# The next sample's 32 compression phases dealt out between the units of a sample's attention

## The reference, cut to what matters

```python
kc = compress_blocks(full_cmp[:, :, 0], cmp_pe[0], cmp_w1[0], cmp_b1[0], cmp_w2[0])
vc = compress_blocks(full_cmp[:, :, 1], cmp_pe[1], cmp_w1[1], cmp_b1[1], cmp_w2[1])
...
p_cmp = masked_softmax(s_c, dist_c >= 0)
o_cmp = jnp.einsum('bghtn,bngd->btghd', p_cmp.astype(vc.dtype), vc)
...
imp = selection_importance(jnp.sum(p_cmp, axis=2), nsb)
...
_, idx = lax.top_k(score, n_sel)
...
o = (gates[:, :, 0, :, :, None] * o_cmp + gates[:, :, 1, :, :, None] * o_slc + gates[:, :, 2, :, :, None] * o_win)
```

## Time and profile before

| | us |
|---|---|
| device time, median of three runs (lowest to highest) | 3484.95 (3482.47 to 3486.91) |
| the profiled execution's own time | 3489.78 |
| its span | 3488.0 |
| TensorE busy | 3230.7 (93%) |
| VectorE busy | 1371.0 (39%) |
| ScalarE busy | 989.5 (28%) |
| GpSimd busy | 922.9 (26%) |
| moved by DMA | 329.68 MB |

### The profile page before, as it was taken

The page is one execution under the profiler, slowest core; times in us unless marked ns, Lnnn a source line. Parts: engine busy times, 40 slices in busy tenths (PEclk is TensorE's granted clock), DMA queues, the critical chain, the costliest instruction groups (busy, mean ns, idle before and its releaser), DMA issues.

```text
span 3488.0 us, 58282 instructions
## 1 busy us (share of the span) xinstructions
PE 3230.7 (93%) x23752; PEld 2946.3 (84%) x23752; DVE 1371.0 (39%) x2939; ACT 989.5 (28%) x1634; POOL 922.9 (26%) x403
## 2 busy tenths in 40 slices
PE   7999998899999999999989999888888887899997
PEld 6999967699998999989987667776677775799997
DVE  3111324411124221241036657766667664411124
ACT  2111210221113211122124444444444443311222
POOL 2333320233334333344220001111111110233332
PEclk9999999999998999989957999899899989899998
DMA  6232221222322223232430004454444544222321
GB/s 140 70 95 73 80 68 52 66 76 70 97 66 76 81 70 97 58 84 70 130 111 1 1 1 152 164 194 160 172 147 156 193 171 120 73 77 80 91 62 35
DMA packets 365938, 329.68 MB, mean 95 GB/s; under 512 B 60469, under 2 KB 345397, under 8 KB 347920
## 3 DMA queue, kind: packets, MB, share of 16 engines
q1 hardware_dynamic: 322264, 180.59, 18.7%
q0 software_dynamic: 21216, 139.89, 11.3%
q10 hardware_dynamic: 22240, 6.17, 0.9%
HBM read 320.39 MB, written 14.58 MB: 96 GB/s over the span
## 4 chain that ended last, share of the span: by engine, by line
PE 79%; issue 8%; DVE 7%; ACT 2%; POOL 1%; DMA 1%; DVEq 0%; POOLq 0%; ACTq 0%
PE psum L1590 51%; PE psum L1854 4%; PE psum L1856 3%; PE psum L1855 3%; PE psum L1910 3%; PE psum L1821 3%; PE psum L2026 2%; PE psum L1943 2%; PE psum L1921 2%; DVE x_lo L1130 1%; PE psum L1874 1%; POOL w_sp L616 1%; PE psum L1584 1%; ACT w_room L913 1%; DMA ring<-in_cache_l_cmp_kv,idxc 1%
## 5 line engine op out<-in xcount | busy, mean ns | idle before, releaser
L1590 PE MATMUL psum<-x_hi,w_sp 128*128 128x288 f32 x5888 | 1042.5, 299 | 38.4 <-DVE x_lo L1130 24.3
L616 POOL TENSOR_TENSOR w_sp<-ring,w_sp 128x2048 fp32r<-128x2048 f32 (+2 forms) x162 | 680.3, 4199 | 1298.9 <-ACT w_sp L759 1298.9
L1590 PEld LDWEIGHTS psum<-x_hi,w_sp 128*128 128x128 f32 x5888 | 880.9, 191 | 43.0 <-issue 23.7
L1590 PE MATMUL psum<-x_lo,w_sp 128*128 128x288 f32 x2944 | 637.5, 299 | 0.0
L1590 PE MATMUL psum<-h_hi,w_sp 128*128 128x288 f32 (+1 forms) x2816 | 502.0, 298 | 0.0
L1590 PEld LDWEIGHTS psum<-x_lo,w_sp 128*128 128x128 f32 x2944 | 481.7, 191 | 0.0
L1590 PEld LDWEIGHTS psum<-h_hi,w_sp 128*128 128x128 f32 (+1 forms) x2816 | 416.5, 188 | 10.5 <-issue 10.1
L1106 DVE TENSOR_TENSOR h_hi<-act_tmp,psum 128x576 f32 (+1 forms) x88 | 66.4, 754 | 861.3 <-ACT act_tmp L798 861.3
L759 ACT ACTIVATE w_sp<-ring 128x2048 fp32r<-128x2048 f32 (+1 forms) x162 | 275.6, 1701 | 445.3 <-PE psum L1590 406.7
L1854 PE MATMUL psum<-ch_hi,w_hi 128*128 128x256 f32 (+1 forms) x1056 | 316.3, 300 | 38.3 <-DVE ch_lo L1263 38.1
L1855 PE MATMUL psum<-ch_lo,w_hi 128*128 128x256 f32 (+1 forms) x1056 | 313.2, 297 | 0.0
(11 more groups left out here) (271 smaller groups left out, 3931.2 us busy)
## 6 DMA issues: line engine op xcount, KB each, us to landing
ring<-in_w_ffn_in SPq DMA_DIRECT2D x168, 512.0 KB
ring<-in_w_ffn_out SPq DMA_DIRECT2D x32, 640.0 KB
ring<-in_w_ffn_out SPq DMA_DIRECT2D x32, 384.0 KB
ring<-in_w_ffn_out SPq DMA_DIRECT2D x32, 320.0 KB
ring<-in_cache_l_win_kv SPq DMA_DIRECT2D x8, 1024.0 KB, 5.5
out<-in_cache_l_win_kv SPq DMA_DIRECT2D x1, 8064.0 KB
ring<-in_w_in_even SPq DMA_DIRECT2D x6, 1024.0 KB
ring<-in_w_in_odd SPq DMA_DIRECT2D x6, 1024.0 KB
```

The lines of the kernel that those rows point to most:

```text
L616: pool.tensor_tensor(w_sp[:, u % 2, 1, 0:w], ring[:, slot, 0:w], w_sp[:, u % 2, 0, 0:w].bitcast(F32), ALU.subtract).then_inc(lo_ready, 1)
L1590: last = pe.matmul(out[:, c], lhsT, rhs[:, c * TH:(c + 1) * TH], start=start, stop=stop)
```

## The change

The work of each sample stays, and its place in the queues moves. While a sample's attention runs, the 32 phases of the *next* sample run between its steps: `PRO = 5` phases at the boundary between two samples, and `PER` phases in the 12 units. The loop now covers six samples, from attention to boundary; the seventh turn and the last attention are written out. The merge of a sample lies in the boundary after it.

```diff
-NSLOT = 6
+NKEY = 3
...
+        PRO = 5
+        PER = [3, 3, 3] + [2] * 9
```

TensorE's new order (`scores` one unit ahead of the output in place of two):

```diff
+            def boundary(b, o, first=False, more=True):
+                keys(b, o, WINC)
+                if more:
+                    phase(b, o + 1, 0)
+                    phase(b, o + 1, 1)
+                pe.wait_ge(q_set, b * 4 + (o * 4 + 4))
+                scores(b, o, 0)
+                if more:
+                    phase(b, o + 1, 2)
+                second_layer(b, o)
+                if more:
+                    phase(b, o + 1, 3)
+                transposes(b, o, 0)
+                if more:
+                    phase(b, o + 1, 4)
+                if not first:
+                    output_transpose(b, o - 1)
...
+            def attend(b, o, more=True):
+                at = PRO
                 for a in range(SU):
+                    if a + 1 < SU:
+                        scores(b, o, a + 1)
+                    for n in range(PER[a]):
+                        if more:
+                            phase(b, o + 1, at)
+                        at += 1
+                        if n == 0:
+                            output(b, o, a)
+                            if a + 2 in CHUNK:
+                                keys(b, o, a + 2)
+                        if n == 1 and a + 1 < SU:
+                            transposes(b, o, a + 1)
```

Beside phase i of the next sample, `along` on ScalarE makes the high part of phase i + 3, and `along` on VectorE turns the chunk of phase i + 3 and makes the low part of phase i + 2. ScalarE copies both halves of the keys (`k_round`, semaphore `k_act`) into one buffer in place of two. Gelu runs twice per sample, on 4 x 255 columns, at the boundary; ScalarE's order there:

```diff
+            def boundary(b, o, first=False, more=True):
+                first_half_of(b, o, 7)
+                k_round(b, o, WINC)
+                gelu_of(b, o, 0)
+                if more:
+                    along(b, o + 1, 0)
+                gelu_of(b, o, 1)
+                if more:
+                    along(b, o + 1, 1)
+                if not first:
+                    weights(b, o - 1)
+                exp_unit(b, o, 0)
```

```diff
+            for s in range(DB):
+                key_load(s, 3)
+                if s + 1 < DB:
+                    chunk_loads(s + 1, 2)
+                    chunk_loads(s + 1, 3)
+                for c in range(4, 8):
+                    key_load(s, c)
+                if s + 2 < DB:
+                    chunk_loads(s + 2, 0)
+                key_load(s, 8)
+                if s + 1 < DB:
+                    key_load(s + 1, 1)
+                    key_load(s + 1, 2)
+                if s + 2 < DB:
+                    chunk_loads(s + 2, 1)
```

More of the change, by code:

```diff
@@ L705, in _ @@
             pool.wait_ge(idx_ready, 5)
[L707 to L739, removed]
+            def gather(dst, rows, at, full):
+                pool.indirect_dma_start(out=dst, out_offset=None, in_=rows,
+                                        in_offset=bass.IndirectOffsetOnAxis(ap=at, axis=0)).then_inc(full, 16)
@@ new lines, in _ @@
+            pool.wait_ge(hb_ready, 1)
+            pool.wait_ge(w1_high, 2)
+            pool.wait_ge(w1_low[0], 1)
+            pool.wait_ge(w1_low[1], 1)
+            chunk_loads(0, 0)
+            pool.wait_ge(blk_done, blk_pos["odd"] + 11)
+            chunk_loads(0, 1)
+            for c in range(2):
+                pool.wait_ge(kv_out[c], 6 * 16)
+            key_load(0, 1)
+            pool.wait_ge(t_ready, R0)
+            key_load(0, 2)
+            chunk_loads(0, 2)
+            chunk_loads(0, 3)
@@ L1040, in _ @@
+            for i in range(3):
+                high_chunk(0, 0, i)
+            for i in range(XS):
+                along(0, 0, i)
+            boundary(0, 0, first=True)
+            with act.Fori(0, DB - 2) as b:
+                attend(b, 0)
+                boundary(b, 1)
+            attend(DB - 2, 0, following=False)
+            boundary(DB - 2, 1, more=False)
+            attend(DB - 2, 1, more=False)
+            weights(DB - 1, 0)
             norm(4, after=3)
@@ L1556, in _ @@
+            for i in range(3):
+                turn(0, 0, i)
+            for i in range(2):
+                low(0, 0, i)
+            for i in range(XS):
+                along(0, 0, i)
+            boundary(0, 0, first=True)
+            with dve.Fori(0, DB - 2) as b:
                 step.off = b * STEPS
                 n_before = step.n
-                attend(b, False)
-                compress(b, 1)
-                first_keys(b, 1)
+                attend(b, 0)
+                boundary(b, 1)
@@ L2085, in _ @@
-            compress(0, 0)
-            with pe.Fori(0, DB - 1) as b:
-                attend(b)
-                compress(b, 1)
-            attend(DB - 1)
-            output_transpose(DB - 1)
+                    each, n = key_count(c)
+                    pe.wait_ge(key_full[c % NKEY], b * each + (o * each + n))
+                if a == 4:
+                    pe.wait_ge(imp_done, b + (o + 1))
+                pe.wait_ge(k_act, b * SR + (o * SR + 2 * c))
+                for gp in range(2):
+                    for p in range(4):
+                        last = pe.transpose(bank(gp)[:, p * P:(p + 1) * P],
+                                            key_slots[c % NKEY][:, p * ROW + gp * P:p * ROW + (gp + 1) * P], ident)
+                    last.then_inc(t_ready, 1)
@@ new lines, in scores @@
+            def scores(b, o, a):
+                pe.wait_ge(soft, b * SU + (o * SU + NU + a - 1))
+                for gp in range(2):
+                    if a == CMPU:
+                        w, rhs = NB, kc[:, gp, :]
+                        pe.wait_ge(cv_sb, b * 2 + (o * 2 + 3))
+                    elif a in CHUNK:
+                        w, rhs = 512, kTc[:, gp, :]
+                        pe.wait_ge(k_act, b * SR + (o * SR + 2 * CHUNK[a] + gp + 1))
+                    else:
+                        w, rhs = DT, kT[:, 0 if a == SLCN else 1, gp, bass.ds(b * DT + (TP + o * DT), DT)]
+                    if a in (WINN, SLCN):
+                        last = pe.matmul(bank(4 + a % 2)[:, 0:w], qb[:, gp, :], rhs, start=gp == 0, stop=gp == 1)
+                    else:
+                        rows = slice(gp * 64, (gp + 1) * 64)
+                        last = pe.matmul(bank(4 + a % 2)[rows, 0:w], qb[:, gp, rows], rhs, start=True, stop=True)
+                last.then_inc(sc_ready, 1)
@@ new lines, in parts, with transposes @@
+            def parts(a):
+                if a == CMPU:
+                    return [(P, 0, P), (NB - P, P, NB - P)]
+                if a in CHUNK:
+                    return [(P, p * P, P) for p in range(4)]
+                return [(DT, 0, DT)]
+            def transposes(b, o, a):
+                n = o * SU + NU + a
+                if a == CMPU:
+                    pe.wait_ge(p_norm, b + (o + 1))
+                else:
+                    pe.wait_ge(p_ready, b * SU + (n + 1))
+                pe.wait_ge(pt_sb, b * SU + n)
+                for j, (m, c0, w) in enumerate(parts(a)):
+                    last = pe.transpose(bank(6)[0:m, j * P:(j + 1) * P], sp3[:, a % 3, c0:c0 + w], ident)
+                last.then_inc(ptp_ready, 1)
@@ L2092, in _ @@
+            pe.wait_ge(soft, NU)
+            for i in range(XS):
+                phase(0, 0, i)
+            boundary(0, 0, first=True)
+            with pe.Fori(0, DB - 2) as b:
+                attend(b, 0)
+                boundary(b, 1)
+            attend(DB - 2, 0)
+            boundary(DB - 2, 1, more=False)
+            attend(DB - 2, 1, more=False)
+            output_transpose(DB - 1, 0)
             pe.wait_ge(ot_done, DB + 1)
```

587 lines of the change are left out of this document (282 added, 305 removed).

## The result

The changed kernel takes 3404.43 us (median of four runs, 3400.93 to 3409.14), the kernel before 3483.78 us beside it: a ratio of 0.977, 95% interval 0.9755 to 0.9789. The forecast was 3403 us. The profiled execution took 3409.1 us, its span 3407.3, TensorE's mean clock 0.946.

The account below looks back on a forecast made before the run. The sample loop, 862.3 us, was taken to lose 25 us of each 107.6 us period to waiting or half clock. Periods of 96 us bring it to 780 us, 82 less, so 3403 us; 8-in-10 range 3345 to 3460 us.

Parts of the forecast that it names:

- The stage: Sample loop, 862.3 to 780 us: first compression 51.1, first turn 87, five of 96, seventh 92, last attention 70.
- rival 4: Phases among attention work: no overlap, TensorE waits for phases as for units; 107 us a period, 3485 us; chance 0.04.
- Units 5 to 11 are TensorE's: Later attention units: TensorE sets the time, 6.1 us per full unit, 39 us in all.
- The boundary and units 0 to 4 are VectorE's, 53 us: Start of a period: VectorE's 41 us of work plus four added waits make 53 us; TensorE has some 45.
- The wait for the weights: Boundary: VectorE waits 4.6 us for ScalarE's merge weights, an 8.6 us chain less 4 us of VectorE work.
- rival 2: Boundary chain longer, with Gelu at 2.0 us and hops of 0.4: 103 us a period, 3456 us; chance 0.20.
- The jump: Loop's jump back to its start: 3.6 us each, placed on VectorE's chain at the boundary.
- rival 1: Whole period: TensorE becomes the bound if weights come early and hops overlap; 88 us a period, 3343 us; chance 0.17.
- Three key slots just fit; piece 8 is 2 us late: Key gathers: landing 6.1 us at the median fits a 6.1 us unit; piece 8, behind two chunk gathers, some 2 us late.
- Rival 3: Pieces 4 to 8: late key slots decide, slower; at an 11 us landing time 884 us of stage, 3507 us; chance 0.09.
- The rule that spoke against it: Key gathers beside VectorE's phases: VectorE's two-port mode locks out GpSimd's descriptor writing; rows show 0.2 us at the median.
- The last attention: Final sample, no phases to hide behind: pieces 4 to 8 take 5.2 us each; 70 us, where 57.8 was.

Follow-up runs that it names:

- the weights' runs: Changed kernel with ScalarE making the merge's weights ahead of Gelu: 3367.88 us (0.9671 of the kernel before); with TensorE's loop also written out: 3358.87 us (0.9649).
- e8: Changed kernel with all three engines' loops written out, chunk gathers behind piece 8 and merge weights ahead of Gelu: 3334.50 us, 0.959 of the kernel before.
- e3: Changed kernel with GpSimd's two chunk gathers issued behind piece 8 instead of ahead of it: 3386.60 us, 0.9724 of the kernel before.
- e6: Changed kernel with the merge's weights made ahead of Gelu at the boundary, loops kept: 3367.88 us, 0.9671 of the kernel before.
- e10: Changed kernel with merge weights ahead of Gelu and chunk gathers behind piece 8, all loops kept: 3351.39 us, 0.9615 of the kernel before.

## Why the prediction was right, and where it was not

- *The stage.* Right in sum and in each of its five rows (table above). That the total is met to 1.4 us is luck: two traces of the changed kernel have turns of 96.2 and 95.2 us. The rest of the kernel did not move: 3489.8 - 862.3 = 2627.5 us before, 3409.1 - 782.5 = 2626.6 us after.
- *The overlap brings the gain* (rival 4 against it). Right: undone, the kernel is slower than before.
- *Units 5 to 11 are TensorE's.* Right: an output follows the last by 6.1 us where no piece is late, VectorE is busy 24.4 of 42.3 us (forecast 26).
- *The boundary and units 0 to 4 are VectorE's, 53 us.* Right in size and, by the weights' runs, right that VectorE's chain sets the end; but its parts were sized wrongly against each other. The wait for the weights was put at 4.6 us; it measures 2.85 us, with 1.17 more for a high part behind Gelu, and taking both away gave 4.8. Gelu took 1.15 us for the 1.1 forecast, where rival 2 had 2.0. Unit 1's exponential (0.8 us) costs nothing, since a phase's parts lie in it. The jump (3.6 us) was put on VectorE; it is TensorE's, and what it costs comes through the waits behind it (1.02 and 1.27 us of VectorE's) and the half clock. For that 1 us was added; 0.06 x 52.75 = 3.2 us of clock are missing in the stretch, of which 1.1 fall in the idle time (0.13 x 8.29), so some 2 us of TensorE's work. These errors nearly cancel: that 53 came out so exactly is luck. The trace of the kernel before had the sign: there too TensorE has a wait without releaser behind the jump, up to the scores of the window.

```profile
2354.00 1.96 PE L2026 MATMUL psum<-big 128*64 128x512 f32 x3 [2.35 <-issue]
```

- *TensorE has only some 45 us of work there, VectorE 41.* Right: with the waits gone the stretch takes 45.1 us with 41.3 us of VectorE. So rival 1 named the limit, with 88 us a turn where e8 has 85.5. This kernel did not stand there, but three small edits away; TensorE's work was put at 83 us, and in e8's turn above it takes 84.2.
- *Three key slots just fit; piece 8 is 2 us late.* Right in size: 2.5 us where piece 7 is on time, else 1.2 beside 0.9 to 1.4 for piece 7. Right in cause for piece 8, which lands behind the two chunk gathers, and by e3 is on time without them. Piece 7's lateness was not forecast. Rival 3 did not come: pieces 4 to 6 of the change keep TensorE waiting 0.2 us at most in its seven turns, but for one wait of 1.8.
- *The rule that spoke against it.* The key gathers into the extra slots took 1.12 us to issue in the kernel before. Now that most lie beside phases, 39 of them take 0.936 us at the median (0.932 to 0.990). The lock that the Trainium skill tells of ("SBUF — State Buffer", "SBUF: two separate sides") does not show in these issues; what it does to a transfer's descriptors these runs do not separate. Nine of the ten chunk gathers that start behind a wait for VectorE's transposes still take 1.12 us, so an effect of VectorE's work on an issue is not ruled out.
- *What was to show it.* VectorE at 70% of a turn (66.3 of 95.0 us) and TensorE's clock above 0.95 (0.96) came out; five jumps of 3.6 us on VectorE did not.
- *The last attention.* 72.2 us for 70; its pieces come 6.7 us late in sum, and the forecast's cycle of slot and unit had that in it, with 5.2 us where 4.7 are measured from piece to piece.

## What to carry to other kernels

When two chains of work are woven into one order, list what each engine's queue must wait for at the seam: here a few small exponentials put behind two table loads and two Gelu instructions held three engines, and moving them ahead was worth 34 us, nearly half as much again as the whole change had brought. An engine's work in a stretch (VectorE 41 us, TensorE 45) says how short it can become; the order says how long it is. And a gather that is issued in time can still be late if another that nobody needs yet was issued just before it.

## What the runs showed of the hardware that was not expected

TensorE's jump back to the loop's start costs 3.6 us of idleness in the change and 2.0 us in e6, and in all ten jumps TensorE goes on 1.6 to 1.8 us after the end of a 16 KB packet of the queue `instruction`. Behind the longer one the granted clock was 0.50 for 4.7 us of work; behind the shorter one the stretch had 1.00 in all five turns of e6, but 0.96 in two of five of e10. Piece 8's gather of 1 MB, which lands in 5.4 to 6.0 us alone, took 7.9 to 8.4 us behind two others.
